# Expert layer of a decoder kernel: the change of experts rotated, and the weights divided in whole chunks of 2048 columns in three buffers

## The reference

```
def swiglu(h, w1, w3, w2):
    return (jax.nn.silu(h @ w1) * (h @ w3)) @ w2

def moe_ffn(h, w_router, w1, w3, w2):
    logits = (h @ w_router).astype(jnp.float32)
    top_v, top_i = lax.top_k(logits, TOP_K)
    top_w = jax.nn.softmax(top_v, axis=-1)
    gate = jnp.sum(jax.nn.one_hot(top_i, N_EXPERTS, dtype=jnp.float32) * top_w[..., None], axis=-2).astype(h.dtype)
    y = jnp.zeros_like(h)
    for e in range(N_EXPERTS):
        y = y + gate[..., e:e + 1] * swiglu(h, w1[e], w3[e], w2[e])
    return y
```

## Time and profile before

| | us |
|---|---|
| median of 3 runs | 2096.97 |
| lowest and highest | 2095.56, 2097.12 |
| the profiled execution, its own time | 2103.66 |
| its span, first to last instruction | 2101.9 |
| PE busy in it | 1977.0 (94%) |
| DVE busy in it | 1524.3 (73%) |
| ACT busy in it | 1218.4 (58%) |
| mean granted clock of PE | 0.970 |

### The profile page before, as it was taken

The page is one execution under the profiler, slowest core; times in us unless marked ns, Lnnn a source line. Parts: engine busy times, 40 slices in busy tenths (PEclk is TensorE's granted clock), DMA queues, the critical chain, the costliest instruction groups (busy, mean ns, idle before and its releaser), DMA issues.

```text
span 2101.9 us, 28303 instructions
## 1 busy us (share of the span) xinstructions
PE 1977.0 (94%) x9524; PEld 1567.4 (75%) x9524; DVE 1524.3 (73%) x1841; ACT 1218.4 (58%) x1574; POOL 89.4 (4%) x133
## 2 busy tenths in 40 slices
PE   4999999899987999999699999999999999999996
PEld 2777787677775777787587787877878778788784
DVE  2755575745456655566599899898998989989897
ACT  2544554343433544543278676786767867678674
POOL 0510000000001310000000000000000000000000
PEclk8999999899998999999799999999999999999998
DMA  9655535265654564544299898998989989899893
GB/s 329 210 214 194 208 121 179 83 220 180 223 178 141 202 221 161 181 140 141 89 336 358 306 365 323 328 355 305 365 324 327 356 303 365 325 325 357 304 357 144
DMA packets 275187, 532.82 MB, mean 253 GB/s; under 512 B 10720, under 2 KB 23216, under 8 KB 274992
## 3 DMA queue, kind: packets, MB, share of 16 engines
q1 hardware_dynamic: 275120, 531.91, 71.7%
HBM read 530.83 MB, written 1.05 MB: 253 GB/s over the span
## 4 chain that ended last, share of the span: by engine, by line
PE 85%; DVE 8%; ACT 3%; issue 2%; DVEq 1%; DMA 1%; SPq 0%; ACTq 0%
PE pA L687 18%; PE pA L689 18%; PE pA L688 18%; PE pO L692 7%; PE pO L687 6%; PE pO L689 5%; PE pO L688 5%; PE pT L735 4%; DVE w_lo L1636 2%; PE pT L692 2%; PE pA L692 2%; ACT w_hi L1277 1%; DMA raw<-in_ada_w 1%; DVE yacc L2182 1%; DVEq L2147 0%
## 5 line engine op out<-in xcount | busy, mean ns | idle before, releaser
L1636 DVE TENSOR_TENSOR w_lo<-raw,w_hi 128x1024 fp32r<-128x1024 f32 x914 | 1092.4, 1226 | 294.7 <-ACT w_hi L1277 273.7
L1277 ACT ACTIVATE w_hi<-raw 128x1024 fp32r<-128x1024 f32 x914 | 957.4, 1059 | 560.5 <-PE pA L689 429.7
L687 PE MATMUL pA<-w_hi,x_lo 128*128 128x512 f32 x896 | 360.8, 403 | 3.6 <-DVE x_lo L2139 3.6
L689 PE MATMUL pA<-w_hi,x_hi 128*128 128x512 f32 x896 | 354.9, 396 | 0.0
L688 PE MATMUL pA<-w_lo,x_hi 128*128 128x512 f32 x896 | 354.6, 396 | 0.0
L687 PE MATMUL pA<-w_hi,h_lo 128*128 128x512 f32 (+2 forms) x736 | 299.8, 407 | 8.4 <-DVE w_lo L1636 8.3
L688 PE MATMUL pA<-w_lo,h_hi 128*128 128x512 f32 (+2 forms) x736 | 289.5, 393 | 0.0
L689 PE MATMUL pA<-w_hi,h_hi 128*128 128x512 f32 (+2 forms) x736 | 289.2, 393 | 0.0
L687 PE MATMUL pO<-w_hi,aT_lo 128*128 128x512 f32 x536 | 213.9, 399 | 13.7 <-DVE yacc L2044 8.8
L688 PE MATMUL pO<-w_lo,aT_hi 128*128 128x512 f32 x536 | 212.4, 396 | 0.0
L689 PE MATMUL pO<-w_hi,aT_hi 128*128 128x512 f32 x536 | 212.4, 396 | 0.0
(11 more groups left out here) (229 smaller groups left out, 1691.0 us busy)
## 6 DMA issues: line engine op xcount, KB each, us to landing
raw<-in_moe_w SPq DMA_DIRECT2D x336, 1024.0 KB, 5.5
raw<-in_w_in SPq DMA_DIRECT2D x56, 1024.0 KB, 5.6
raw<-in_ada_w SPq DMA_DIRECT2D x48, 1024.0 KB, 9.4
raw<-in_ffn_w SPq DMA_DIRECT2D x33, 1024.0 KB, 5.5
raw<-in_w_out SPq DMA_DIRECT2D x8, 1024.0 KB, 5.1
raw<-in_cmp_k_w SPq DMA_DIRECT2D x4, 1024.0 KB, 5.6
raw<-in_cmp_v_w SPq DMA_DIRECT2D x4, 1024.0 KB, 10.4
raw<-in_w_read_nsa SPq DMA_DIRECT2D x4, 1024.0 KB, 8.4
```

The lines of the kernel that those rows point to most:

```text
L687: nc.tensor.matmul(dst, xl, wh, start=first, stop=False, skip_group_check=True)
L689: return nc.tensor.matmul(dst, xh, wh, start=False, stop=last, skip_group_check=True)
L1277: return nc.scalar.activation(dst, src, ACT.Copy)
L1636: V.tensor_tensor(w_lo[m][:, 0:n], raw[s][:, i * n:(i + 1) * n], w_hi[m][:, 0:n].bitcast(F32), ALU.subtract).then_inc(raw_done, 1)
```

## The change

The weights of the experts are divided a whole chunk at a time. ACT writes 2048 columns of `wide_hi` in one instruction, DVE 2048 columns of `wide_lo` in one, in three buffers. Two of them lie where the four `w_hi` and four `w_lo` buffers lie, the third in the place of `h_hi` and `h_lo`, the layer's input, which the experts do not read. The counts stay in halves: each of the wide instructions raises its semaphore by two.

The look-ahead no longer runs from the mixing part into the experts. Instead ACT divides two chunks behind the mixing part (`start_wide`), and DVE one behind the modulation and one in the middle of the router's arithmetic.

`gather` of the next expert moves into the fifth block of the seven (the third in `rest`), between U and `down`. `turn_sel` moves into the third block (the first in `rest`), likewise between U and `down`; it turns `sel` itself, and `sel_s` is gone. `scatter` and `open_outs` move into an expert's second block, between its U and `down`. The output is divided too: ACT rounds both halves of `pO` into `oe_hi`, DVE makes `oe_lo`, and `scatter` takes two float32r products for each of its four results; two of them go to `pA[1]` and `pA[3]` in place of the two `pT` banks. The inner loop over blocks is written out.

`wide_to` in the diff is ACT's; DVE has the same with the subtraction. The last two pieces are DVE's.

```diff
+WIDE = 3
...
+            def wide_half_in(i):
+                h = b.hl.take()
+                if i == 0:
+                    b.raw.take()
+                    b.wide.take()
+                    pe.wait_ge(raw_done, b.hl.done(h + 1))
+                slot, at = b.wide.slot(b.wide.n - 1), slice(i * HALF, (i + 1) * HALF)
+                return wide_hi[slot][:, at], wide_lo[slot][:, at]
...
-                            turned([sel_s[:, t, :]], P)
+                            turned([sel[:, t, :]], P)
...
-                    def block():
+                    def block(between=None):
                         gate_up(pA[0], G, g_free)
                         turn_a()
                         gate_up(pA[2], U, u_free)
+                        hidden_in()
+                        if between is not None:
+                            between()
                         down()
...
                     def scatter():
                         evacuated(b.O, O_free, 2)
+                        v = gv.take()
+                        pe.wait_ge(gather_free, gv.done(v - 1))
                         for t in range(TT):
                             for half in range(2):
-                                dst = take_T()
-                                mm(dst[:, :], selT[:, t * P:(t + 1) * P], oe[:, half * W:(half + 1) * W]).then_inc(T_full, 1)
+                                dst = pA[1 + 2 * half] if t else take_T()
+                                at = slice(half * W, (half + 1) * W)
+                                mm(dst[:, :], selT[:, t * P:(t + 1) * P], oe_lo[:, at], True, False)
+                                mm(dst[:, :], selT[:, t * P:(t + 1) * P], oe_hi[:, at], False, True).then_inc(gather_full if t else T_full, 1)
+                    def rest(more):
+                        block(turn_sel)
+                        block()
+                        block(gather if more else None)
+                        block()
+                        block()
...
                         gather()
                         first_block()
                         gate_up(pA[2], U, u_free)
-                        gather()
-                        turn_sel()
-                        with rounds(pe, 0, NE - 1, {b.raw: 42, b.hl: 84, b.T: 20, b.O: 2, G: EFB, U: EFB, av: EFB, xv: 1, gv: 1, sv: 1}):
-                            blocks()
+                        block(open_outs)
+                        with rounds(pe, 0, NE - 1, {b.raw: 42, b.hl: 84, b.wide: 42, b.T: 18, b.O: 2, G: EFB, U: EFB, av: EFB, xv: 1, gv: 2, xg: 1}):
+                            rest(True)
                             first_block()
                             turn_a()
                             gate_up(pA[2], U, u_free)
+                            hidden_in()
                             down(True)
-                            gather()
-                            scatter()
-                            turn_sel()
-                        blocks()
+                            block(scatter_open)
+                        rest(False)
                         turn_a()
+                        hidden_in()
                         down(True)
                         scatter()
...
+            def wide_to(at):
+                while b.hl_in.n < min(at, b.end):
+                    b.hl_in.take()
+                    h = b.hl_in.take()
+                    g, m = b.raw.slot(b.raw.take()), b.wide_in.slot(b.wide_in.take())
+                    act.wait_ge(landed[g], (b.raw.before(b.raw.n - 1) + 1) * 16)
+                    act.wait_ge(half_used, b.hl_in.done(h - 2 * WIDE))
+                    copy(wide_hi[m][:, :], raw[g][:, :]).then_inc(hi_ready, 2)
+            def use_wide(n):
+                wide_to(b.hl.n + 2 * n + 4)
...
-                b.end = 2 * (DEPTH * MIX_CHUNKS + DENSE_CHUNKS + NE * 6 * EFB)
+                b.end = 2 * (DEPTH * MIX_CHUNKS + DENSE_CHUNKS)
...
+                    start_wide()
+                    wide_to(b.hl_in.n + 2)
...
                     V.tensor_scalar(r(0), r(4), 2.0, None, ALU.is_lt).then_inc(sel_ready, 1)
+                    wide_to(b.hl_in.n + 2)
```

More of the change, by code:

```diff
@@ L1585, in outs @@
[L1585 to L1590, removed]
-                    with rounds(act, 0, passes, {b.raw: 42 * NE, b.hl: 84 * NE, b.hl_in: 84 * NE, b.T: 20 * NE, b.O: 2 * NE, G: EFB * NE,
-                                                 gv: NE + 1}) as p:
-                        hi_x()
-                        use(2)
-                        silu()
-                        use(2)
-                        keep_sel()
-                        with rounds(act, 0, NE - 1, {b.raw: 42, b.hl: 84, b.hl_in: 84, b.T: 20, b.O: 2, G: EFB, gv: 1}):
-                            blocks(True)
+                        use_wide(2)
@@ new lines, in block, with outs, rest @@
+                        if between is not None:
+                            between()
+                    def outs():
+                        act.wait_ge(half_used, b.hl.done(b.hl.n - 1))
+                        for half in range(2):
+                            v = b.O.take()
+                            copy(oe_hi[:, half * W:(half + 1) * W], pO[b.O.slot(v)][:, :]).then_inc(oe_hi_ready, 1)
+                    def rest(more):
+                        block(keep_sel)
+                        use_wide(2)
+                        for _ in range(3):
+                            block()
+                            use_wide(2)
+                        block(hi_x if more else None)
+                        use_wide(2)
@@ L1659, in start_splits, with wide_to, start_wide, use_wide @@
             def start_splits():
[L1661 removed]
+                b.end = 2 * (DEPTH * MIX_CHUNKS + DENSE_CHUNKS)
                 split_to(AHEAD)
[L1664 to L1668 removed]
+            def wide_to(at):
+                while b.hl_in.n < min(at, b.end):
+                    b.hl_in.take()
+                    h = b.hl_in.take()
+                    g, m = b.raw.slot(b.raw.take()), b.wide_in.slot(b.wide_in.take())
+                    dve.wait_ge(hi_ready, b.hl_in.done(h))
+                    V.tensor_tensor(wide_lo[m][:, :], raw[g][:, :], wide_hi[m][:, :].bitcast(F32), ALU.subtract).then_inc(raw_done, 2)
+            def start_wide():
+                b.end += 2 * NE * 6 * EFB
+            def ahead():
+                n = b.end - b.hl_in.n + 4
+                b.end += 4
+                wide_to(b.hl_in.n + n)
+            def use_wide(n):
+                wide_to(b.hl.n + 2 * n + 4)
+                for _ in range(n):
+                    b.hl.take()
+                    v = b.hl.take()
+                return v
             def use(n, halves=AHEAD):
@@ new lines, in block, with outs, scattered @@
+                        if between is not None:
+                            between()
+                    def outs(v):
+                        for half in range(2):
+                            at = slice(half * W, (half + 1) * W)
+                            po, free = O_in(v)
+                            dve.wait_ge(oe_hi_ready, ov.done(ov.take()))
+                            V.tensor_tensor(oe_lo[:, at], po[:, :], oe_hi[:, at].bitcast(F32), ALU.subtract).then_inc(free, 1)
+                    def scattered(e, t):
+                        if t:
+                            v = gv.take()
+                        for half in range(2):
+                            if t:
+                                dve.wait_ge(gather_full, gv.done(v, 2) - 1 + half)
+                                pt, free = pA[1 + 2 * half], None
+                            else:
+                                pt, free = T_in()
+                            dst = yacc[:, t, half * W:(half + 1) * W]
+                            ins = V.scalar_tensor_tensor(dst, pt[:, :], gate16[:, t, bass.ds(e, 1)], dst, ALU.mult, ALU.add)
+                            if free is not None:
+                                ins.then_inc(free, 1)
+                        if t:
+                            dve.drain().then_inc(gather_free, 1)
@@ new lines, in rest @@
+                    def rest(e=None):
+                        block(lambda: skip(b.T, 2))
+                        use_wide(2)
+                        if e is not None:
+                            kept = kv.take()
+                            dve.wait_ge(sel_kept, kv.done(kept))
+                            one_hot(e + 1)
+                        block()
+                        use_wide(2)
+                        block()
+                        use_wide(1)
+                        if e is not None:
+                            gathered()
+                        use_wide(1)
+                        block()
+                        use_wide(2)
+                        block(lo_x if e is not None else None)
+                        return use_wide(2)
```

176 lines of the change are left out of this document (89 added, 87 removed).

## The result

The changed kernel takes 2073.7 us, the median of 4 runs (2070.7 to 2078.8), beside 2097.05 for the kernel before in 4 runs of the same comparison (2095.6 to 2100.2). The ratio is 0.9882, with a 95% interval from 0.986 to 0.9904. The prediction was 2071.0. The profiled execution has a span of 2069.0 and an own time of 2071.26, against 2101.9 and 2103.66 before.

The account below looks back on a forecast made before the run. PE bounds the kernel inside an expert (busy 109.84 of 110 us), broken only at changes of experts. Terms of -26.1, -3.6, +3.1, -0.9, +0.9, +0.6 sum to -26.0: 2071.0 us, range 2067 to 2077, with rivals 2064 to 2086.

Parts of the forecast that it names:

- change of experts: Between two experts on PE: 10.20 us without weight products becomes 6.47, 3.73 less each, 7 times: -26.1 us.
- one gather fewer: Before the first expert's blocks: PE makes `gather` eight times instead of nine, -3.6 us.
- `lo_x`: On DVE ahead of the next block's chunk 0: makes it 0.77 late instead of 0.33, 7 times, +3.1 us.
- DVE at the loop's return: Four additions to `yacc` on DVE: taken as hidden by PE's 0.2 to 3.6 us of extra work, no cost.
- the end: At the last `down`: DVE has the whole last chunk ahead of `lo_a`, +0.6 us; the last `scatter` taken as 0.
- ahead of the experts: On DVE: a subtraction gone behind the mixing part, -0.9 us; a wide one added in the router, +0.9 us.
- A plain block's room: At chunk 4 before `down`: the wide division is ready 0.22 us before PE asks, so no stall, 0.
- From the profile to the median: Whole time: profiled execution lies 6.7 us above the median; the same difference taken from 2077.7 gives 2071.0.
- The loop's return: Rival at the loop over experts: PE loads its longer program again at each of 7 returns, up to 2109 us; 5%.
- The pauses: Rival at changes of experts: loads kept up only through the 10 us pauses, so no gain, 2097 us; 5%.
- Chunk 4: Rival in plain blocks: its division comes 0.3 us beyond the room, 39 times, 16 us, giving 2087; 14%.

Follow-up runs that it names:

- the kernel with four additions: The changed kernel with all four additions of the scatter on DVE put between the second block's two divisions; 2068.9 us in one run.
- the second profile: The changed kernel run once more without alteration, on the chip of three follow-up kernels; 2074.22 us, ratio 0.9885.

## Why the prediction came out right

The time was 2.7 above the number, and inside both ranges. The terms didn't all hold; errors of both signs cancelled, and that the sum came out so close is luck. From the two profiles, in the expert stretch:

| step | predicted | measured |
|---|---|---|
| change of experts, 7 times | -26.1 | -29.9 |
| one gather fewer | -3.6 | -3.6 |
| `lo_x`, 7 times | +3.1 | +3.2 |
| DVE at the loop's return | 0 | +2.5 |
| the end | +0.6 | +2.5 |
| ahead of the experts | -0.9 + 0.9 | not in the stretch, see below |
| sum | -26.0 | -25.3 (the stretches: -25.5) |

- **Change of experts: the mechanism right, the size too small.** By the distances between transposes it cost 27.53 - 17.24 = 10.29 before. After, `scatter` with `open_outs` costs 19.49 - 17.24 = 2.25, `gather` 3.56, `turn_sel` 0.21, together 6.02 where the prediction's sum had 6.47. I had counted `open_outs` at 0.51 and three restarts at 0.1 on top of starts that mostly run on without one: 1178.48 to 1178.73 is 0.25. That is 0.45 of the 0.54; the other 0.09 is the change before, 10.29 by the transposes where the sum had 10.20.
- **One gather fewer: right.** Up to the first transposes the stretch is 4.2 shorter, and `open_outs` and `turn_sel`, which stood there too, give back 0.6 in the first expert's next blocks (17.66 and 17.45).
- **`lo_x`: right.** 18.12 in place of 17.66, and in the kernel with the wide divisions alone 18.11.
- **A plain block's room: right.** 0.22 computed, 0.2 found. The prolonged slopes gave 2.28 and 2.01; the rows have 2.29 and 1.92 in length (1.44 to 3.47 us behind E, 2.03, until DVE starts). PE waited at `down` only at the end of the last expert.
- **The sentence that failed** is that "`keep_sel` and the four additions to `yacc` likewise lie in blocks in which PE has 0.2 to 3.6 us of extra work". I looked for cover on PE and did not ask what follows on DVE: two of the additions stand right ahead of the loop's return, and one more 2.2 us division behind them was due. It is 2.5 of the sum (7 returns), and is gone where the four additions stand together.
- **The end: the wait as computed.** 1.97 where the earlier trace rows have 1.31, 0.66 more for 0.6. In the execution of the kernel with four additions, whose end is the same code, the last transposes are 28.6 from the end of the span against 27.8, so +0.8 in all. The rest of the 2.5 is PE's clock in that execution.
- **Ahead of the experts: both terms right.** From the start of the mixing part's last product to the addition it is 0.50 in place of 1.33, -0.8. From the addition to the first expert product it is 36.1 in place of 35.3, +0.8.
- **From the profile to the median: not shown.** The prediction carried the 6.7 us between the profiled execution and the median over. The stretches differ by 25.5, the two profiled executions by 32.4 (7.4 of it ahead of the experts), the medians by 23.4. The lengths ahead of the experts vary by more than the 2.7 by which the number is off.
- **The rivals.** The loop's return did not stall PE: over it the next gate product starts 0.23 behind the last of `down` (1184.27 and 1184.50), and the DMA view above lists no packet of code in 770 us. Of the two things that the Trainium skill, Runtime: NRT & Kernel Launch, section "Instruction fetch mechanics", says of the window, the room for 2048 instructions agrees with this trace; the two pages, with a stall at a branch out of them, don't. That the limit is 2048 no run here shows; 1,227 are kept. The pauses did not feed the buffers: 344 GB/s are kept up and no division waits for a load. Chunk 4 is never late, but one 0.5 us instruction on ACT ahead of it makes it so.

Two things were not in the prediction at all. The gain needs the third buffer's memory: with four halves the period is 2.75 us longer than with six. And the width takes back 1.25 an expert of what the buffer gives, the difference of 127.9 and 126.65. Why the code ahead of the experts, the same in all these kernels, takes up to 13 us more or less from one execution to another stays open; no experiment was made on it.

## What to carry to other kernels

When work is moved from a gap into the full stretch, ask on each engine, not on the bottleneck alone, for how long it is now away from feeding the bottleneck, and compare that with the reserve in buffers: here 2.1 and 2.9 us away against some 1.9 that three halves of 1.4 leave. Buffers and instruction size are separate choices; the same memory in six small buffers did better than in three large ones (126.65 against 127.9), although each small instruction pays its fixed cost. Measure a change of 1% on a period in the middle of the trace, where it repeats to 0.05 us, and not on the whole time, which varied by 5 to 15 us between executions of one kernel.

## What the runs showed of the hardware

**PE's clock fell behind waits, not in every execution.** PE's timeline at the end of the changed kernel, and the windows view on it (the figure ahead of the DMA share is the granted clock):

```profile
2041.28 0.50 PE L696 MATMUL pO<-wide_hi,aT_lo 128*128 128x512 f32 x1 [1.97 <-DVE aT_lo L2244]
...
2042.36 0.63 PE L696 MATMUL pO<-wide_hi,aT_lo 128*128 128x512 f32 x1
2042.79 0.63 PE L697 MATMUL pO<-wide_lo,aT_hi 128*128 128x512 f32 x1
...
2045.26 0.39 PE L697 MATMUL pO<-wide_lo,aT_hi 128*128 128x512 f32 x1
```

```profile
2020.00:2038.00 18.00, 18.00 (x81) 14.46 (x79) 15.67 (x10) 13.30 (x10) 0.00 (x0) 1.00 0.59 217
2041.30:2045.00 3.70, 3.70 (x10) 2.86 (x11) 0.00 (x0) 0.00 (x0) 0.00 (x0) 0.56 0.00 0
```

Products come 0.43 apart in place of 0.23: the lower of the two levels, 1.2 GHz. This fall cost about 1.55 us, and the same code with the same wait of 1.97 ran on at 0.23 in the second profile. Over the profiles with one of these waits ahead of the last `down`: behind 1.97 to 2.01 us the products slowed down in four of seven, behind 1.12 to 1.31 in none of six. At the first products of the experts it is the same: 0.43 apart for about eight of them in the first profiles of before and after (1.5 us), none in the second of after. Such falls explain the 2.6 us between the two expert stretches of one and the same kernel: 1.5 at the first products and 1.2 at the end, where the second execution's fall came later, in the last `scatter`, whose products were 0.43 apart behind a wait of 2.3. None lies in a period.

**The return of a loop on DVE left no gap behind a running division and cost some 0.5 us behind a drain:** 0.79 and 0.72 with both, 0.30 and 0.26 with the drain alone.
